# Moving the mix, the key squares and four sums of a recurrence stage from VectorE and ScalarE to GpSimd

## What is computed

```
zf = z + (0.5 * (prev + nxt) - z) * mu            # centred_shift_mix, 7 tiles of 128 channels
r, k, v, w_lo, a_lo = split(zf)
kk = k * rw_kk;  kk = kk / max(sqrt(sum(kk * kk)), 1e-12)
for d in range(2):                                # forward, backward
    w = -softplus(-(w0[d] + tanh(w_lo) @ w2[d])) - 0.5;  decay = exp(-exp(w))
    a = sigmoid(a0[d] + a_lo @ a2[d]);  kd = k * (1 + (a - 1) * k_a)
    S = S * decay + (S @ -kk) (kk * a)' + v kd';  y[d] = S @ r
    bonus[d] = sum(r * kd * r_k) * v
o = y[0] + y[1]
```

## Time and profile before

| | us |
|---|---|
| median of three runs | 2461.0 |
| the profiled execution | 2462.29 |
| its span | 2460.6 |
| PE, DVE, ACT, POOL busy | 2263.6, 1551.8, 1009.5, 265.3 |
| local part of the recurrence, in the span | 1262.7 to about 1791 |
| mean granted clock of TensorE | 0.969 |

### The profile page before, as it was taken

How to read it: one execution, slowest core, us unless ns; L and a number is a source line. 1 busy time by engine, 2 the same in 40 slices (tenths; PEclk the granted TensorE clock), 3 DMA queues, 4 the chain that set the end, 5 groups by cost and what they waited for, 6 DMA issues and landing times. The chain is left out here.

```text
span 2460.6 us, 66375 instructions
## 1 busy us (share of the span) xinstructions
PE 2263.6 (92%) x26630; PEld 1853.4 (75%) x26630; DVE 1551.8 (63%) x2611; ACT 1009.5 (41%) x1734; POOL 265.3 (11%) x335
## 2 busy tenths in 40 slices
PE   4999999999899999999947899999788799899998
PEld 2788878888688887888836777777657576688887
DVE  5756566666865456665635777777456676856754
ACT  5444234544532123445424555555333666411111
POOL 0000000000000000000031222222124663000000
PEclk7999999999999999999978999999978899999999
DMA  7344333333242333333330111110068523834542
GB/s 240 107 135 125 111 94 111 113 117 102 94 129 93 96 108 97 106 111 119 107 101 25 32 41 32 32 56 17 19 214 305 126 94 95 288 115 171 197 152 88
DMA packets 250306, 277.75 MB, mean 113 GB/s; under 512 B 30683, under 2 KB 174171, under 8 KB 247643
## 3 DMA queue, kind: packets, MB, share of 16 engines
q1 hardware_dynamic: 245306, 266.95, 33.9%
q10 hardware_dynamic: 4576, 8.40, 0.9%
q0 software_dynamic: 320, 0.98, 0.2%
HBM read 184.66 MB, written 91.62 MB: 112 GB/s over the span
## 5 line engine op out<-in xcount | busy, mean ns | idle before, releaser
L715 PE MATMUL proj_ps<-h_hi,w_hi 128*128 128x512 f32 x1656 | 649.5, 392 | 27.6 <-DVE h_lo L465 19.7
L716 PE MATMUL proj_ps<-h_lo,w_hi 128*128 128x512 f32 x1656 | 647.0, 391 | 0.0
L717 PE MATMUL proj_ps<-h_hi,w_lo 128*128 128x512 f32 x1656 | 646.4, 390 | 0.0
L318 ACT CAST w_hi<-w_raw 128x512 fp32r<-128x512 f32 x420 | 255.1, 621 | 694.0 <-PE proj_ps L717 353.2
L715 PEld LDWEIGHTS proj_ps<-h_hi,w_hi 128*128 128x128 f32 x1656 | 312.3, 189 | 98.2 <-issue 26.1
L717 PEld LDWEIGHTS proj_ps<-h_hi,w_lo 128*128 128x128 f32 x1656 | 312.2, 189 | 65.6
L716 PEld LDWEIGHTS proj_ps<-h_lo,w_hi 128*128 128x128 f32 x1656 | 312.4, 189 | 62.9
L482 DVE TENSOR_TENSOR w_lo<-w_raw,w_hi 128x512 fp32r<-128x512 f32 x420 | 283.2, 689 | 44.3 <-ACT w_hi L318 43.7
L498 DVE TENSOR_TENSOR z_slots<-proj_ps,x_rows 128x512 f32<-128x512 f32 x174 | 120.2, 691 | 169.9 <-PE proj_ps L717 167.9
L498 DVE TENSOR_TENSOR x_rows<-proj_ps,x_rows 128x512 f32<-128x512 f32 x116 | 80.1, 691 | 108.9 <-PE proj_ps L717 102.9
L1010 POOL MEMSET rpb_padded<- 60x127 f32 x1 | 0.2, 198 | 1261.3 <-POOLq L89 1261.3
(11 more groups left out here) (380 smaller groups left out, 4101.4 us busy)
## 6 DMA issues: line engine op xcount, KB each, us to landing
w_raw<-in_w_in SPq DMA_DIRECT2D x240, 256.0 KB, 3.0
scratch_gatesT<-z_slots SPq DMA_DIRECT2D x128, 256.0 KB, 2.7
late_rows<-scratch_gatesT SPq DMA_DIRECT2D x64, 512.0 KB, 4.4
scratch_zT<-z_slots SPq DMA_DIRECT2D x108, 256.0 KB, 2.4
ada<-in_ada_w SPq DMA_DIRECT2D x4, 2048.0 KB, 15.2
late_rows<-scratch_zT SPq DMA_DIRECT2D x4, 2048.0 KB, 12.7
late_rows<-scratch_branchT SPq DMA_DIRECT2D x16, 512.0 KB, 5.3
late_rows<-in_x SPq DMA_DIRECT2D x16, 512.0 KB, 4.9
```

The source lines that it names most:

```text
L318: A.copy(wh[:, i, :, :], raw[:, q, :, :]).then_inc(w_hi, 1)
L715: T.matmul(out, wh[:, i, k, :], hi[:, o, k, :], start=(first and k == 0), stop=False, skip_group_check=not first)
L716: T.matmul(out, wh[:, i, k, :], lo[:, o, k, :], start=False, stop=False, skip_group_check=not first)
L717: last = T.matmul(out, wl[:, i, k, :], hi[:, o, k, :], start=False, stop=(k == 3), skip_group_check=not first)
```

## The change

GpSimd takes over the whole mix: neighbours, times half mu, own rows times 1-mu (each one instruction over all seven tiles), and their sum in four instructions (z6, z23, z01, z45). It also squares the keys, makes the two bonus-row operations, adds the identity to P and adds the two directions' y. ScalarE stages P and the backward y by copies from PSUM, and its exps stand earlier. On VectorE, R and K (and kka of a backward next unit) stand ahead of the fifth mask; A is now the last hat. The low-rank weights come by two DMAs a unit instead of a copy from a tile that held both.

```diff
         @block.sync
             def turn(n, more):
+                last = isinstance(n, int) and n == NBLK - 1
                 for d in range(2):
+                    if not (last and d):
+                        prep_p.after(sp, (n + d, 1 - d), "ta")
+                        load_lora(d)
+                    if d == 0 and not first_block(n):
+                        y_out(n - 1)
                     if d and more:
                         load(n + 2)
...
         @block.gpsimd
+            def scaled_neighbours(n):
+                pool.wait_ge(mix_step, n * 3 + 1)
+                G_.tensor_tensor(nbr[:], nbr[:], per_tile(hmu), ALU.mult).then_inc(mix_step, 1)
+            def scaled_own(n):
+                pool.wait_ge(mix_step, n * 3 + 2)
+                G_.tensor_tensor(own, own, per_tile(omu), ALU.mult).then_inc(mix_step, 1)
+            def mixed_tiles(n, name, j, k):
+                mix_g.done(G_.tensor_tensor(zf[:, j:k, :], nbr[:, j:k, :], own[:, j:k, :], ALU.add), 0, name)
+            def bonus_rows(n):
+                prep_v.after(pool, (n, 1), "kd")
+                keys_g.done(G_.tensor_tensor(kds[:], kd[:, 0], kd[:, 1], ALU.add), 1, "kds")
+                keys_g.after(pool, (n, 1), "kds")
+                prep_a.after(pool, (n, 0), "rrk1")
+                keys_g.done(G_.tensor_tensor(kds[:], kds[:], rrk[:], ALU.mult), 1, "bt")
+            def add_identity(n, d):
...
+                for c in range(2):
+                    last = G_.tensor_tensor(to[:, c], pst[:, c].rearrange("p g (m j) -> p g m j", m=2), eye, ALU.add)
+            def add_y(n):
+                main_a.after(pool, (n, 1), "Y1.")
+                G_.tensor_tensor(yst[:], yst[:], yst2[:], ALU.add).then_inc(y_added, 1)
             def prologue():
...
                 neighbours(0)
+                pool.wait_ge(consts_set.sem, 8)
+                scaled_neighbours(0)
+                scaled_own(0)
+                pool.wait_ge(mix_step, 3)
+                for name, j, k in (("z6", 6, 7), ("z23", 2, 4)):
+                    mixed_tiles(0, name, j, k)
+                key_squares(0)
+                for name, j, k in (("z01", 0, 2), ("z45", 4, 6)):
+                    mixed_tiles(0, name, j, k)
...
+                neighbours(1)
+                scaled_neighbours(1)
             def unit(n, d, nxt):
                 head_v.after(pool, (n, d), "MB.")
                 main_g.done(nc.gpsimd.tensor_tensor(tiled(Z[:]), tiled(MB[:]), eight(lev0[:, d, :]), ALU.mult), d, "Z.")
+                if d and nxt:
+                    key_squares(n + 1)
+                    mixed_tiles(n + 1, "z01", 0, 2)
+                    prep_v.after(pool, (n, 1), "bonus")
+                    mixed_tiles(n + 1, "z45", 4, 6)
...
+                    main_a.after(pool, before, "P.")
+                    main_g.done(add_identity(*before), d, "P.")
+                    if d == 0:
+                        add_y(n - 1)
...
                 main_g.done(nc.gpsimd.tensor_copy(tiled(X0[:]), eight(i64[:, :])), d, "X0.")
-                if d == 0 and not (isinstance(n, int) and n == NBLK - 1):
-                    neighbours(n + 1)
-                prep_p.after(pool, nxt, "ta")
-                pool.sem_inc(pool_go, 1)
-                main_g.done(nc.gpsimd.tensor_copy(lora[:], lora_of[:, d, :]), d, "lora.")
+                if d == 0:
+                    if more:
+                        scaled_own(n + 1)
+                        prep_p.after(pool, nxt, "ta")
+                        pool.wait_ge(mix_step, n * 3 + 6)
+                        mixed_tiles(n + 1, "z6", 6, 7)
+                    bonus_rows(n)
+                    if more:
+                        mixed_tiles(n + 1, "z23", 2, 4)
+                elif not (isinstance(n, int) and n >= NBLK - 2):
+                    neighbours(n + 2)
+                    scaled_neighbours(n + 2)
                 main_p.after(pool, (n, d), "G5.")
                 main_g.done(nc.gpsimd.tensor_copy(tiled(MB[:]), eight(i64[:, :])), d, "MB.")
...
         @block.vector
+            def hats_early(n, d):
+                prep_a.after(dve, (n, d), "tot")
...
+                done(V.tensor_tensor(chunks(AR[:, 1, :, :]), chunks(zf[:, 0:2, :]), padded(d, 1 - d), ALU.mult), "R")
+                prep_v.after(dve, (n, d), "kd")
+                done(V.tensor_tensor(Kh[:], kd[:, d], EN[:], ALU.mult), "K")
+                if d:
+                    done(V.scalar_tensor_tensor(kka[:], aa[:], 1.0, kk[:], ALU.add, ALU.mult), "kka")
             def last_products(n, d, done):
-                main_p.after(dve, (n, d), "PQ.")
+                main_a.after(dve, (n, d), "P.")
...
-                    done(V.tensor_tensor(to(Pst), pq[:, :, 0, :, :], eye, ALU.add), f"P{c}.")
             def unit(n, d, nxt):
...
                     if v == 4 and nxt:
                         if d:
                             norms(nxt[0])
                         rates(*nxt)
-                        if d == 0:
-                            bonus_rows(n)
+                        hats_early(*nxt)
...
         @block.scalar
                 if nxt:
                     key_rates(*nxt)
+                    if d:
+                        exps(*nxt)
+                        bonus_keys(nxt[0])
                 factor(X[:], "X4.", 4)
                 factor(Z[:], "Z4.", 0)
+                if nxt and d == 0:
+                    exps(*nxt)
                 main_p.after(act, (n, d), "A.")
                 own(A.copy(eights(WI[:, :, :, :, 0:CH]), ps[:, 6:8, 0:256].rearrange("p q (k t) -> p q k t", t=CH)), "At.")
-                if nxt:
-                    exps(*nxt)
...
+                if d == 0 and not (isinstance(n, int) and n == NBLK - 1):
+                    tanh_lo(n + 1)
+                    raw_keys(n + 1)
+                main_p.after(act, (n, d), "PQ.")
+                main_g.after(act, (n, d), "P.")
+                own(A.copy(pst[:], ps[:, 0:2, :].rearrange("p c (g i k) -> p c g i k", g=2, i=2)[:, :, :, 0, :]), "P.")
         @block.tensor
             def first_scores(u, back):
-                prep_v.after(pe, u, "B", back)
+                prep_v.after(pe, u, "A", back)
...
             E = U
             pe.wait_ge(centre_set, 1)
-            pe.wait_ge(lora_set, 1)
+            pe.wait_ge(lora_in, 32)
```

More of the change, by code:

```diff
@@ L841, in __init__ @@
         for d in range(2):
-            ends = [self.at[r] - 1 for r in self.made[d][1:]] + [self.each + self.at[self.made[1 - d][0]] - 1]
+            if not self.made[d]:
+                self.adds.append({})
+                continue
+            first = self.each + self.at[self.made[1 - d][0]] if self.made[1 - d] else 2 * self.each + self.at[self.made[d][0]]
+            ends = [self.at[r] - 1 for r in self.made[d][1:]] + [first - 1]
             self.adds.append({r: e - self.at[r] + 1 for r, e in zip(self.made[d], ends)})
@@ L925, in recurrence_local_stage @@
[L925 to L929, removed]
+        U = 32
+        newton = ["nx", "n0"] + [f"n{i}{x}" for i in range(3) for x in "abc"] + ["rx"]
@@ new lines, in recurrence_local_stage @@
+        prep_v = Turns(ctx, nc, "prep_vector", ["lw", "L", "Lx", "inc"] + newton + ["kd", "R", "K", "kk", "kka", "B", "A", "bonus"], U,
+                       leaves_out=(("Lx", "inc", "bonus"), newton + ["kk"]))
+        prep_a = Turns(ctx, nc, "prep_scalar", ["th", "kkr0", "kkr1", "tw0", "tw1", "ta0", "ta1", "u0", "u1", "EI", "EN", "tot", "rrk0", "rrk1"], U,
+                       leaves_out=((), ("th", "kkr0", "kkr1", "rrk0", "rrk1")))
+        mixed, keys = ["z6", "z23", "ksq", "z01", "z45"], ["kds", "bt"]
@@ L987, in _ @@
             load(1)
+            prep_p.after(sp, (0, 0), "ta")
+            load_lora(1)
             sp.wait_ge(rpb_in, 16)
@@ L1064, in unit @@
                 main_g.done(nc.gpsimd.tensor_copy(tiled(MB[:]), eight(i64[:, :])), d, "MB.")
-            units(pool, prologue, unit)
+            prologue()
+            unit(0, 0, (0, 1))
+            unit(0, 1, (1, 0))
+            with hinted_loop(nc, pool, 1, NBLK - 2) as n:
+                unit(n, 0, (n, 1))
+                unit(n, 1, (n + 1, 0))
+            unit(NBLK - 2, 0, (NBLK - 2, 1))
+            unit(NBLK - 2, 1, (NBLK - 1, 0))
+            unit(NBLK - 1, 0, (NBLK - 1, 1))
+            unit(NBLK - 1, 1, None)
+            main_a.after(pool, (NBLK - 1, 1), "P.")
+            add_identity(NBLK - 1, 1).then_inc(pool_go, 1)
+            add_y(NBLK - 1)
         N_MASKS = 1 + 8 * len(LEVELS) + 2 * 5 + 2
@@ L1291, in bonus_keys @@
             def bonus_keys(n):
-                prep_v.after(act, (n, 0), "mix1")
+                mix_g.after(act, (n, 0), "z01")
                 for p in range(2):
@@ L1412, in key_sums @@
             def key_sums(u, back):
-                prep_v.after(pe, u, "ksq", back)
+                mix_g.after(pe, u, "ksq", back)
                 for g in range(2):
@@ L1463, in beside @@
                         if more:
-                            main_g.after(pe, u, "lora.", 1)
```

(1 more changed line is left out.)

153 lines of the change are left out of this document (61 added, 92 removed).

## The result

The changed kernel takes 2568.8 us (median, 2565.9 to 2571.4) against 2462.0 for the kernel before in the same session: 1.043 times, 95% interval 1.0412 to 1.0448, so 107 us slower. The profiled execution took 2568.4 us, its span is 2566.7.

What follows compares the result with a forecast made beforehand. TensorE, busy nine tenths of the local stage's steady part, was taken as the bound. Forward 8x4.0+2.3, backward 7x7.5-0.1, clock 8, start 4 and end 4.5 summed to +103 us: 2564 us, range 2474 to 2585 (0.9).

Steps and rivals of the forecast that it cites:

- The likeliest case: Whole kernel: running GpSimd reads block VectorE's instructions with two SBUF operands for their whole length; 2564 us, chance 0.56.
- Hold on VectorE: VectorE instructions with two SBUF operands wait out a whole running GpSimd instruction; backward mask and Z5 move some 7.7 us.
- Backward unit: Backward units n = 0 to 6: GpSimd's neighbours, product and reset delay mask and Z5; +7.5 us each, -0.1 without contention.
- the clock: TensorE after a backward pause of 7 us: half clock costs 1.2 us each, +8 over seven.
- Forward unit: Forward units: fifth mask behind three hats, plus contention with GpSimd; +4.0 us each, +2.3 in the last block, +1.9 without contention.
- the forward clock: TensorE after forward pauses of 4.4 us: half clock costs up to +10 us more, left out of the sum.
- Start and end: Start: two mask sums each wait for a GpSimd instruction, +4 us; end: work queued after PQ, +4.5 us.
- GpSimd yielding: Rival: VectorE is never held, or only briefly, and GpSimd's MB reset comes late instead; 2509 us, chance 0.18.
- no contention: Rival: GpSimd and VectorE meet without any cost worth naming; 2481 us, chance 0.19.
- the early exps: Rival: ScalarE's earlier exps deliver tot in time, so the kernel is not slower; 2455 us, chance 0.06 with its variant.

Runs made afterwards that it cites:

- order-only run: Kernel before with R, K (and kka of a backward next unit) ahead of the fifth mask, A last, ScalarE's exps ahead; GpSimd and mix unchanged: 2502.8 us.

## Why the prediction was right, step by step

- **Total.** 2564 us was predicted, 2568.8 measured. The sum gave +103 for the profiled execution; its local part shows +108.9, and -2.9 came from the rest, whose time drifts. The likeliest case was the one that came. Its mechanism is confirmed by taking each half away; that the total is so close is partly luck (below).
- **Hold on VectorE.** This was the step named as most likely wrong, argued from one row of the other direction. It holds: 0.43 to 3.31 us and 0.69 to 3.66. The place was right (copy of the norm rows, `k_d`), since SP's wait for `ta` set the landing of z as worked out. One forecast of how it would look was not met: durations of 0.7 us with gaps. The durations themselves grew.
- **Backward unit.** Hold and order: +7.5 predicted; the clock +1.2 beside it; +7.9 measured for both. From `ta` to Z5 were 9.49 us in the earlier trace rows and are 17.0 now; 18.4 were predicted. The missing 1.4 is the mis-sized hold, 6.3 us (2.88 on the copy, 2.97 on `k_d`, 0.40 on R) and not 7.7: the product of 1792 elements with half mu took 3.24 us, not 4.0 (extrapolated from smaller sizes, although the sum of the same size stood in the earlier trace rows with 3.17), and the reset of `m_b` held R only in part. From Z5 to GY it is 5.6 us (1633.37 to 1638.95) where the earlier trace rows and the prediction's 1622.93 give 4.5: that is the clock, of about the size allowed for.
- **Forward unit.** +4.0 predicted, +5.4 measured. R starts 3.1 us after `k_d` (2.9 predicted), the hold added 1.7 (0.33 on R, 0.98 on K, 0.41 on kka; 2.2 predicted), and Z5 comes 7.45 us after `k_d` instead of 3.07: 4.4 late, where 2.4 and 2.2 more for the hold were worked out. What failed is the term left out of the sum, the forward clock: bonus at 2.07 us instead of 1.13, and 5.6 us from Z5 to GY instead of the 4.0 worked out. "Up to +10" for nine units had been set aside for it; the forward units came 13 over the sum. The order-only run shows how much that matters: there the forecast, which had no clock in it, was 21 us against 45.7.
- **Why did the total fit, then?** Partly by luck: forward units cost 47 us where 34 were summed, backward units 57 where 60 (with the clock) were, start and end 5 where 8.5 were, and the rest came 2.9 us shorter. An error of 13 us one way and three that add to 10 the other way.
- **Start and end.** +4 and +4.5 predicted. Z of the first unit comes at 1311.78 against 1309.1 in the earlier trace rows, +2.7. The masks were done near 1304.9, as worked out. The mask sums met the neighbour sum, 3.87 us for two where 1.01 stood in the earlier trace rows (first fence below): both waited for this one instruction, +2.9 us, where each was to wait for one of two. Z then stood behind the product with half mu in GpSimd's queue (1308.51 to 1311.82). The first unit took 29.7 us against 25.7, no more than the later forward units grew by. The end: +1.5, not +4.5. From PQ's end to the local end the prediction had 6.2 us, and it is 6.2 (1894.8 to 1900.96, last fence and local end); but it set this against VectorE's last products at 1788.8 and not against the local end of before, 1792.03, which also stood 4.6 behind PQ. The wrong step is the mark in the trace of before.

```profile
1304.91 3.87 DVE L1270 TENSOR_TENSOR level_masks<-level_masks,ident 128x320 f32<-128x320 f32 x2 [6.22 <-POOL level_turned L1097]
...
1304.95 3.48 POOL L1024 TENSOR_TENSOR neighbours<-z_halo 128x1792 f32<-128x1792 f32 x1
```

```profile
1894.48 0.33 PE L1449 MATMUL rw_ps<-v_rows,k_rows 64*64 64x64 f32 x8
```

- **Rivals.** GpSimd yielding (2509) and no contention (2481) are refuted by VectorE's durations of 3.3 and 3.7 us above; the early exps did not deliver, since `tot` still comes 2.4 us after VectorE could use it and R stands before the mask.

## What to carry to other kernels

GpSimd's idle time is not free room beside a VectorE that is on the critical path: in these traces a long GpSimd instruction that reads SBUF stopped the VectorE instructions with two SBUF operands that started beside it, and a copy and a scalar step in SBUF, until it ended. So place it where VectorE works from PSUM or waits anyway, and perhaps split it, which no run here tried. Before moving an operation ahead of the one that the critical path waits for, ask what *its own* input waits for; a ready operation ahead costs its length, an unready one costs its wait as well. And price a new pause of TensorE with the half clock that may follow it (1.2 us a forward unit here), or fill it with a product that is ready.

## What the runs showed of the hardware that was not expected

- A GpSimd *fill* held a single-operand VectorE copy (1.74 us beside a fill of 1.59, 0.43 alone) but no two-operand instruction (0.67 and 0.68 beside fills).
- A VectorE `TENSOR_SCALAR` from and to SBUF, 0.42 us alone, took 2.73 us beside GpSimd's neighbour sum: having one operand was no protection here, and an operand in PSUM was (the mask, 0.68 us beside the running product).
- Two pauses of TensorE as short as 1.05 and 1.36 us, 0.6 us apart, were followed by half clock in most units of the order-only kernel, but not in (1, 0) and (2, 0); with a product of 1.02 us in the second pause no unit's bonus product slowed down any more.
- On GpSimd a two-operand instruction of 1792 elements took 3.17 to 3.24 us (1.8 ns an element), the sum of two views of one tile and the product with a broadcast operand alike, where one of 512 takes 1.27 (2.5 ns) and one of 1024 2.35 (2.3 ns). Why an element is cheaper in the long ones, no run shows.
